# Keys and values of the memory projected in pieces between the steps of two attentions

## The chip, the cores and the metric

The kernel runs on one core of a Trainium2 chip. The metric is the device time of one execution in microseconds (us), as the median of several runs. The program is one launch on that core.

## The reference, cut to what matters

One input x of 256 rows by 1024 passes through two transformer blocks. The part in question is the start of the first block. Everything is float32.

```python
xn = rmsnorm(h, g_mix);  z = xn @ w_in                 # q, k, v: 8 heads of 64; pool input 512; 8 forget logits
fox = forgetting_attention(q, k, v, f_logit)           # causal, with sums of log-sigmoids added to the scores
pool = multiscale_pool(p_in, w_pool, pool_scale)       # trailing means over 2, 4, 8, 16 rows, then a linear map
h = h + concat([fox, pool]) @ w_out

hn = rmsnorm(h, g_mem_q);   mn = rmsnorm(mem, g_mem_kv)
mq  = rmsnorm(heads(hn @ w_mem_q), g_q_mem)            # 4 heads of 128
mkv = mn @ w_mem_kv                                    # first 512 columns: keys, last 512: values
mk  = rmsnorm(heads(mkv[:, :512]), g_k_mem);  mv = heads(mkv[:, 512:])
mo  = softmax(mq @ mk.T / sqrt(128)) @ mv
h = h + mo @ w_mem_out                                 # then the feed-forward layer, and the second block
```

The memory `mem` (256 rows by 1024) is an input of its own: its norm, keys and values depend on nothing that x goes through, and they are first needed by the scores and products of the memory attention.

## The kernel before

Rows stand in two blocks of 128 (`tb` 0 and 1), the 1024 features in eight tiles of 128, or two halves of four. Weights come as slabs of 128 by 2048 floats (1 MB) through a ring of four slots (`NSLOT`): slab n uses slot n modulo 4. SyncE loads it, ScalarE rounds it to a high part (`hi`, L1001), VectorE subtracts to get the low part (`lo`, L1367), and TensorE multiplies. A float32 product is three matmuls on the short type: high by high, high by low, low by high (`mm3`). One slab with both row blocks is 24 matmuls of 512 columns; one projection of 512 columns is two slabs, 48 matmuls. The next load into a slot waits until the old low part is made; the next rounding waits until TensorE has used the old slab. Activations are split in the same way into `x_hi` and `x_lo`.

A norm is: squares on ScalarE (`norm_squares`), mean on VectorE (`x_variance`), the power -1/2 on GpSimd (L407), scaling on VectorE (`x_scale`), transposes on TensorE (`x_transposes`, L416), gain on VectorE (`x_full`), then high part on ScalarE (`x_hi`) and low part on VectorE (`x_low`). `normed_chunk` puts the transposes of the second row block between the first matmuls. `head_norm` does the same per head, with the sum of squares reduced on VectorE.

Nothing is scheduled by a program: each engine has its list of instructions, written out by hand, and takes them in this order. An instruction waits for semaphores, and all that stands behind it on its engine waits too. The order on TensorE before is: memory's norm and its four slabs (keys, then values) with the transposes of the keys; x's norm and the eight slabs of `w_in`, with the forget gates behind the first two; head transposes; pooling (averages, projection); scores of the forgetting attention, first for row block 1, then 0 (`fox_scored`); transposes of the weights, products with the values (`fox_mixed`); the four slabs of `w_out`; the memory query's norm, two slabs, head transposes, scores, transposes, value products (`mem_mixed`); two slabs of `w_mem_out`; and the feed-forward layer. VectorE and ScalarE go along, and split slabs ahead between the steps. `memory attention` means the part from the query's norm to `mem_mixed`, `seam` a place where TensorE has finished a residual's product and waits for the norm of the sum.

Every name `mem_...`, `fox_...` or `x_...` in quotes is a semaphore; some share one counter, in the order of the table `IN_ORDER`.

## Time and profile before

| | us |
|---|---|
| median of 3 runs | 1440.93 |
| lowest and highest | 1439.89, 1443.88 |
| the profiled execution | 1439.54 |
| its span | 1438.2 |
| TensorE matmul busy | 1374.4 (96%) |
| VectorE busy | 966.8 (67%) |
| ScalarE busy | 624.1 (43%) |

The first product starts 15.50 us into the span, and the first product with `w_mem_out` at 207.02. In the timeline a row has its start, its duration, the engine, the line, the operation, what it writes and reads, its shape and how many instructions were merged in it; in brackets stand the time for which the engine was idle before and what ended it. Durations of matmuls overlap, so the distance from one start to the next is what a matmul costs. A float32 matmul that isn't split shows as two rows. In a row of a table by stretches each engine has busy time and count; the granted clock of TensorE is the first number behind POOL's, as a share of 2.4 GHz.

### The profile page before, as it was taken

Reading aid. Unit: us, or ns where it says so; the run is one execution under the profiler, and the core shown is the slowest. Engines: PE = TensorE matmul, PEld = TensorE weight load, DVE = VectorE, ACT = ScalarE, POOL = GpSimd, SP = SyncE. Lnnn points to the kernel's source line nnn. Section 1 sums busy time; section 2 is a strip of 40 time slices with the busy share of each in tenths; the row PEclk is TensorE's granted clock in tenths of the full one; section 3 lists DMA queues with packets and bytes.
Section 4 is the critical chain, followed back from the end, with each engine's and each line's share of the span. In section 5 each row is a group of like instructions: output and inputs, shape, how many; then the busy total and the mean of one; then the engine's idle time right before and its main releaser. Section 6 shows DMA issues by size and latency. Waiting matters only on the chain.

```text
span 1438.2 us, 19599 instructions
## 1 busy us (share of the span) xinstructions
PE 1374.4 (96%) x8222; PEld 1224.7 (85%) x8222; DVE 966.8 (67%) x1543; ACT 624.1 (43%) x535; POOL 35.1 (2%) x31
## 2 busy tenths in 40 slices
PE   6897868999999999899999999999999999999998
PEld 5786657888888888699999999999998888888886
DVE  6434645888846585758887869999546666666664
ACT  5344334434323855344444444444444444444441
POOL 0010010000002000000000000000000000000000
PEclk9899979999988998999999999999999999999999
DMA  7440226899724221355666748888898777777760
GB/s 309 156 170 1 117 85 245 325 375 377 288 96 190 88 89 59 149 191 202 224 234 220 244 169 255 250 253 257 261 319 316 267 294 302 279 290 296 291 263 30
DMA packets 83239, 317.39 MB, mean 221 GB/s; under 512 B 6096, under 2 KB 40144, under 8 KB 53200
## 3 DMA queue, kind: packets, MB, share of 16 engines
q1 hardware_dynamic: 83152, 316.14, 60.9%
q8 instruction: 65, 1.06, 0.3%
q14 instruction: 22, 0.18, 0.0%
HBM read 281.51 MB, written 34.60 MB: 220 GB/s over the span
## 4 chain that ended last, share of the span: by engine, by line
PE 93%; DVE 3%; ACT 3%; issue 0%; DMA 0%; POOL 0%; DVEq 0%; ACTq 0%; POOLq 0%
PE psum L413 91%; PE psum L416 2%; DVE arena L1406 1%; DVE slab_lo L1367 0%; ACT arena L1092 0%; ACT x_hi L1015 0%; DMA arena<-in_mem 0%; POOL statistics L407 0%; ACT slab_hi L1001 0%; DVE residual L1435 0%; ACT arena L1004 0%; DVE arena L1402 0%; DVE arena L1422 0%; DVE statistics L1419 0%; DVE statistics L1511 0%
## 5 line engine op out<-in xcount | busy, mean ns | idle before, releaser
L1367 DVE TENSOR_TENSOR slab_lo<-slab_raw,slab_hi 128x2048 fp32r<-128x2048 f32 x207 | 471.7, 2288 | 250.5 <-ACT slab_hi L1001 240.9
L1001 ACT ACTIVATE slab_hi<-slab_raw 128x2048 fp32r<-128x2048 f32 x207 | 394.1, 1911 | 350.7 <-PE psum L413 350.7
L413 PE MATMUL psum<-x_hi,slab_hi 128*128 128x256 f32 x1184 | 338.3, 286 | 0.9 <-ACT arena L1187 0.9
L413 PE MATMUL psum<-slab_hi,x_hi 128*128 128x512 f32 x784 | 316.3, 403 | 22.5 <-ACT x_hi L1015 13.1
L413 PE MATMUL psum<-x_hi,slab_lo 128*128 128x256 f32 x1184 | 335.2, 283 | 0.0
L413 PE MATMUL psum<-x_lo,slab_hi 128*128 128x256 f32 x1184 | 335.2, 283 | 0.0
L413 PE MATMUL psum<-slab_lo,x_hi 128*128 128x512 f32 x784 | 311.8, 398 | 0.0
L413 PE MATMUL psum<-slab_hi,x_lo 128*128 128x512 f32 x784 | 311.6, 397 | 0.0
L413 PEld LDWEIGHTS psum<-x_hi,slab_hi 128*128 128x128 f32 x1184 | 227.3, 192 | 1.7 <-ACT arena L1187 1.2
L413 PEld LDWEIGHTS psum<-x_lo,slab_hi 128*128 128x128 f32 x1184 | 227.3, 192 | 0.0
L413 PEld LDWEIGHTS psum<-x_hi,slab_lo 128*128 128x128 f32 x1184 | 227.2, 192 | 0.0
L413 PEld LDWEIGHTS psum<-slab_hi,x_hi 128*128 128x128 f32 x784 | 151.6, 193 | 57.5 <-ACT x_hi L1015 14.7
L413 PEld LDWEIGHTS psum<-slab_hi,x_lo 128*128 128x128 f32 x784 | 151.0, 193 | 32.5
L413 PEld LDWEIGHTS psum<-slab_lo,x_hi 128*128 128x128 f32 x784 | 151.5, 193 | 30.9 <-issue 0.2
L413 PE MATMUL psum<-slab_hi,weighted_hi 128*128 128x512 f32 x280 | 109.9, 393 | 1.4 <-DVE weighted_lo L1582 1.4
L413 PE MATMUL psum<-slab_hi,weighted_lo 128*128 128x512 f32 x280 | 109.1, 390 | 0.0
L413 PE MATMUL psum<-slab_lo,weighted_hi 128*128 128x512 f32 x280 | 109.0, 389 | 0.0
L1332 ACT ACTIVATE arena<-psum 128x1024 f32<-128x1024 f32 x32 | 32.8, 1025 | 127.7 <-PE psum L413 127.7
L1923 DVE TENSOR_SCALAR arena<-iota,selected_first_keys,selected_gates 128x128 f32<-128x128 f32 x256 | 86.9, 339 | 0.0
L413 PEld LDWEIGHTS psum<-slab_hi,weighted_hi 128*128 128x128 f32 x280 | 52.6, 188 | 12.2 <-DVE weighted_lo L1582 1.6
L413 PEld LDWEIGHTS psum<-slab_hi,weighted_lo 128*128 128x128 f32 x280 | 52.6, 188 | 11.0
L413 PEld LDWEIGHTS psum<-slab_lo,weighted_hi 128*128 128x128 f32 x280 | 52.6, 188 | 10.5
(233 smaller groups left out, 1188.8 us busy)
## 6 DMA issues: line engine op xcount, KB each, us to landing
slab_raw<-in_ex_u SPq DMA_DIRECT2D x64, 1024.0 KB, 6.1
slab_raw<-in_ex_v SPq DMA_DIRECT2D x64, 1024.0 KB, 4.8
arena<-in_w_ada SPq DMA_DIRECT2D x24, 1024.0 KB, 6.4
slab_raw<-in_w_in SPq DMA_DIRECT2D x22, 1024.0 KB, 5.6
slab_raw<-in_w_gu SPq DMA_DIRECT2D x22, 1024.0 KB, 7.1
hidden_store<-arena SPq DMA_DIRECT2D x32, 512.0 KB, 7.3
gates_store<-arena SPq DMA_DIRECT2D x8, 2048.0 KB, 9.6
arena<-hidden_store SPq DMA_DIRECT2D x32, 512.0 KB, 5.7
```

The lines of the kernel that those rows point to most:

```text
L413: return PE.matmul(out, lhsT, rhs, start=start, stop=stop)
L416: return PE.transpose(out, in_, ident[0:in_.shape[0], 0:in_.shape[0]])
L1001: ACTE.activation(slab_hi[:, slot, :], raw[:, slot, :], ACT.Copy).then_inc(hi_made[slot], 1)
L1332: ACTE.activation(hidden_out[c % 2], banks(2 * (c % 2), 2).rearrange("p (a t) -> p a t", a=EX_A), ACT.Gelu).then_inc(sem("hidden_made"), 1)
L1367: DVE.tensor_tensor(slab_lo[:, slot, :], raw[:, slot, :], slab_hi[:, slot, :].bitcast(f32), ALU.subtract).then_inc(lo_made[slot], 1)
L1406: ins = DVE.tensor_scalar(full[:, k], src[:, k], gain[:, kk:kk + 1], shift[:, kk:kk + 1], ALU.mult, ALU.add)
L1923: ins = DVE.tensor_scalar(gated[n][:, j, :], iota[:], sel_a[:, t], sel_g[:, t], ALU.is_equal, ALU.mult)
```

## The change

The weight slabs come in another order: `w_in` first, then the two slabs of memory's keys (now 8 and 9), `w_out`, `w_mem_q`, the two slabs of memory's values (16 and 17) and `w_mem_out`. The program begins with x. Memory is loaded after the third slab, in one transfer; its norm stands beside the forget gates and in the third slab of `w_in`. The first four of memory's feature tiles are kept in `weighted_hi` and `weighted_lo`; the last four are split twice, for the keys into the first half of `x_hi` and `x_lo`, for the values into the second. The 96 matmuls with memory come in eight pieces of 12 (one slab, one row block): one before and one after the pool's projection, two behind the scores of the forgetting attention, two behind the memory query's projection, one before and one after the memory scores. The keys are copied out of PSUM, normed in place and transposed between the second and third slab of `w_out`. The scores of row block 0 lie closer together in PSUM, so that banks 6 and 7 are free for the pieces. The arena is laid out anew, and the counters are renumbered.

```diff
 def slab_order():
-    order = [("w_mem_kv", j) for j in range(4)] + [("w_in", j) for j in range(8)]
+    order = [("w_in", j) for j in range(8)] + [("w_mem_kv", j) for j in range(2)]
     order += [("w_out", 2 * c + half) for half, c in OUT_ORDER]
-    order += [("w_mem_q", j) for j in range(2)] + [("w_mem_out", j) for j in range(2)]
...
+S_IN, S_MK, S_OUT, S_MQ, S_MV, S_MO, S_FF, S_IN2, S_OUT2, S_PQ, S_EU, S_EV, S_END = (
+    0, 8, 10, 14, 16, 18, 20, 53, 67, 71, 79, 143, 207)
...
-                SP.dma_start(gm[:, tb], a["mem"][:, tb]).then_inc(sem(f"mem_loaded{tb}"), 16)
+                SP.dma_start(h[:, tb], a["x"][:, tb]).then_inc(sem(f"x_loaded{tb}"), 16)
             SP.dma_start(cols[:, 0:192], a["cols"]).then_inc(sem("columns_loaded"), 16)
             SP.dma_start(ident[:], a["ident"]).then_inc(sem("columns_loaded"), 16)
             SP.dma_start(ones[:], a["ones"]).then_inc(sem("columns_loaded"), 16)
             SP.dma_start(iota[:], a["iota"]).then_inc(sem("columns_loaded"), 16)
-            for n in range(4):
+            for n in range(3):
                 load(n)
-            SP.dma_start(h[:], a["x"]).then_inc(sem("x_loaded"), 16)
-            for n in range(4, 8):
-                load(n)
-            SP.wait_ge(*after("x_scaled", 2))
             SP.dma_start(wsm, a["w_f"]).then_inc(sem("forget_weight_loaded"), 16)
             SP.dma_start(fox_mask, a["fox_mask"]).then_inc(sem("block1_constants_loaded"), 16)
             SP.dma_start(upto, a["upto"]).then_inc(sem("block1_constants_loaded"), 16)
             SP.dma_start(bfor, a["b_forget"]).then_inc(sem("block1_constants_loaded"), 16)
-            load(8)
-            load(9)
+            SP.dma_start(gm, a["mem"]).then_inc(sem("mem_loaded"), 16)
+            for n in range(3, 6):
+                load(n)
             SP.wait_ge(*after("x_transposed", 4 * MIX + 4))
             SP.dma_start(bandsT, a["bands"]).then_inc(sem("pool_tables_loaded"), 16)
             SP.dma_start(zs[:, 0:512], a["w_pool"]).then_inc(sem("pool_tables_loaded"), 16)
-            for n in range(10, S_FF + 2):
+            for n in range(6, S_FF + 2):
...
-            normed_chunk(4, S_KV, MEM, 0)
-            gemm_chunk(6, S_KV + 2)
-            PE.wait_ge(*after("mem_k_normed", 1))
-            head_transposes("mem_k_transposed", lambda hh, tb: mkn[:, tb * MEM_H + hh, :], MEM_H, 0, P)
-
-
-            PE.wait_ge(*after("mem_kT_made", 2))
-            PE.wait_ge(*after("mem_v_copied", 1))
             normed_chunk(0, S_IN, MIX, 4)
             PE.wait_ge(*after("forget_weight_lo", 1))
             small_products().then_inc(sem("forget_products_made"), 1)
+            x_transposes(MEM, 4, 0)
             PE.wait_ge(*after("forget_logs_made", 1))
             PE.wait_ge(*after("block1_constants_loaded", 48))
             mm(ps[:, 7, 16:24], upto, fl[:, 0, :])
             mm(ps[:, 7, 24:32], ones[:], fl[:, 0, :], True, False)
             mm(ps[:, 7, 24:32], upto, fl[:, 1, :], False, True).then_inc(sem("forget_sums_made"), 1)
-            gemm_chunk(2, S_IN + 2)
+            for half in range(2):
+                take(S_IN + 2 + half)
+                for tb in range(TB):
+                    half_products(2, S_IN + 2 + half, half, tb)
+                if half == 0:
+                    PE.wait_ge(*after("x_full", 4 * MEM + 2))
+                    x_transposes(MEM, 2, 1)
+            PE.wait_ge(*after("x_full", 4 * MEM + 4))
             gemm_chunk(4, S_IN + 4)
             PE.wait_ge(*after("forget_sums_copied", 1))
             gemm_chunk(6, S_IN + 6)
 
+
+            def memory_products(n, half, tb):
+
+                if half == 0:
+                    ah, al = wh, wl
+                elif n < S_MV:
+                    ah, al = xh[:, 0:4], xl[:, 0:4]
+                else:
+                    ah, al = xh[:, 4:8], xl[:, 4:8]
+                if tb == 0:
+                    take(n)
+                bh, bl = parts(n % NSLOT, 4, 512)
+                for k in range(4):
+                    ins = mm3(ps[:, 6 + tb, :], ah[:, k, tb * P:tb * P + P], al[:, k, tb * P:tb * P + P], bh[:, k], bl[:, k],
+                              half == 0 and k == 0, half == 1 and k == 3)
+                if tb == TB - 1:
+                    used(ins, n)
...
+            PE.wait_ge(*after("fox_kT_made", 4))
+            PE.wait_ge(*after("mem_early_lo", 1))
+            memory_products(S_MK, 0, 0)
             PE.wait_ge(*after("pool_average_copied", 1))
             for g in range(4):
                 ins = mm(ps[:, 2 + g // 2, (g % 2) * S:(g % 2) * S + S], zs[:, g * P:g * P + P], mixT[:, g, :])
             ins.then_inc(sem("pool_projected"), 1)
+            memory_products(S_MK, 0, 1)
...
+            PE.wait_ge(*after("mem_late_lo_for_k", 1))
+            for tb in range(TB):
+                memory_products(S_MK + 1, 1, tb)
...
+            PE.wait_ge(*after("mem_k_normed", 1))
+            head_transposes("mem_k_transposed", lambda hh, tb: mkn[:, tb * MEM_H + hh, :], MEM_H, 4, P)
...
             normed_chunk(0, S_MQ, MEMQ, 4)
+            for tb in range(TB):
+                memory_products(S_MV, 0, tb)
             PE.wait_ge(*after("mem_q_normed", 1))
             head_transposes("mem_q_transposed", lambda hh, tb: mqn[:, tb * MEM_H + hh, :], MEM_H, 2, P)
+            PE.wait_ge(*after("mem_late_lo_for_v", 1))
+            memory_products(S_MV + 1, 1, 0)
             PE.wait_ge(*after("mem_qT_made", 2))
+            PE.wait_ge(*after("mem_kT_made", 2))
...
+            memory_products(S_MV + 1, 1, 1)
             for tb in range(TB):
                 PE.wait_ge(*after("mem_weights_made", tb + 1))
                 for mb in range(TB):
+                    if mb == 1:
+                        PE.wait_ge(*after("mem_exp_made", 2 * MEM_H))
...
-            x_hi(MEM, 0)
+                ACTE.wait_ge(*after(f"x_loaded{tb}", 16))
+                norm_squares(MIX, 0, tb)
+            x_hi(MIX, 0)
             hi(0, 1)
-            x_hi(MEM, 1)
-            hi(2, 3)
-            ACTE.wait_ge(*after("x_loaded", 16))
-            for tb in range(TB):
-                norm_squares(MIX, 2, tb)
-            hi(4, 5)
-            slab_done(ACTE, S_KV + 1)
-            ACTE.wait_ge(*after("x_lo_made", 4 * MEM + 4))
-            ACTE.activation(mksq, banks(4, 2).rearrange("p (h d) -> p h d", d=MEM_D), ACT.Square).then_inc(
-                sem("mem_k_squared"), 1)
-            slab_done(ACTE, S_KV + 3)
-            ACTE.activation(mv, ps[:, 6:8, :], ACT.Copy).then_inc(sem("mem_v_copied"), 1)
-            ACTE.wait_ge(*after("columns_loaded", 64))
-            heads_out("mem_k_transposed", mkT, MEM_H, 0, P, cols[:, C_MEMK:C_MEMK + 1], "mem_kT_made")
-
-
-            for tb in range(TB):
-                x_hi(MIX, tb)
+            x_hi(MIX, 1)
             ACTE.wait_ge(*after("forget_weight_loaded", 16))
             ACTE.activation(wsm_h[:], wsm, ACT.Copy).then_inc(sem("forget_weight_hi"), 1)
-            hi(6, 7)
+            hi(2)
+            for tb in range(TB):
+                ACTE.wait_ge(*after("mem_loaded", 16))
+                norm_squares(MEM, 2, tb)
+            hi(3, 4, 5)
+            slab_done(ACTE, S_IN + 1)
+            ACTE.wait_ge(*after("x_lo_made", x_part(MIX, 1, 1)))
+            ACTE.activation(qsq, banks(0, 2).rearrange("p (h d) -> p h d", d=FOX_D), ACT.Square).then_inc(
+                sem("fox_q_squared"), 1)
             ACTE.wait_ge(*after("forget_added", 1))
             log_sigmoid_rest(fl, fe).then_inc(sem("forget_rest_made"), 1)
-            hi(8, 9)
-            slab_done(ACTE, S_IN + 1)
-            ACTE.wait_ge(*after("x_lo_made", 4 * MIX + 4))
-            ACTE.activation(qsq, banks(0, 2).rearrange("p (h d) -> p h d", d=FOX_D), ACT.Square).then_inc(
-                sem("fox_q_squared"), 1)
-            hi(10, 11)
+            hi(6)
+            ACTE.wait_ge(*after("x_full", 4 * MEM + 3))
+            ACTE.activation(wh[:], mem_early, ACT.Copy).then_inc(sem("mem_early_hi"), 1)
...
+            ACTE.wait_ge(*after("x_full", 4 * MEM + 4))
+            ACTE.activation(xh[:, 0:4], mem_late, ACT.Copy).then_inc(sem("mem_late_hi_for_k"), 1)
...
+            slab_done(ACTE, S_MK + 1)
+            ACTE.activation(mkn.rearrange("p (b h) d -> p b (h d)", b=TB), ps[:, 6:8, :], ACT.Copy).then_inc(
+                sem("mem_k_copied"), 1)
...
-            hi(14, 15, 16, 17)
+            ACTE.wait_ge(*after("mem_k_copied", 1))
+            ACTE.activation(mksq, mkn, ACT.Square).then_inc(sem("mem_k_squared"), 1)
+            hi(12, 13)
+            ACTE.wait_ge(*after("columns_loaded", 64))
+            heads_out("mem_k_transposed", mkT, MEM_H, 4, P, cols[:, C_MEMK:C_MEMK + 1], "mem_kT_made")
+            hi(14, 15)
...
+            ACTE.activation(xh[:, 4:8], mem_late, ACT.Copy).then_inc(sem("mem_late_hi_for_v"), 1)
+            hi(18)
...
+            slab_done(ACTE, S_MV + 1)
+            ACTE.activation(mv, ps[:, 6:8, :], ACT.Copy).then_inc(sem("mem_v_copied"), 1)
...
-            hi(20, 21)
+            hi(19, 20, 21)
...
+            def memory_low(name, dst, hi_, full):
+                DVE.wait_ge(*after(name.replace("_lo", "_hi"), 1))
+                DVE.tensor_tensor(dst, full, hi_.bitcast(f32), ALU.subtract).then_inc(sem(name), 1)
...
+            lo(2)
+            k = [x_variance(MEM, 2, tb) for tb in range(TB)]
+            for tb in range(TB):
+                x_scale(MEM, 2, tb, k[tb])
...
+            for half in range(2):
+                x_full(MEM, 4, 0, half, cols[:, CKV:CKV + 8], None)
...
-            lo(14, 15, 16, 17)
+            lo(12)
+            head_norm("mem_k", mkn, mkn, 8, MEM_D, 40, mksq, (13,))
+            lo(14, 15)
...
+            lo(16, 17)
+            head_norm("mem_q", banks(0, 2).rearrange("p (h d) -> p h d", d=MEM_D), mqn, 8, MEM_D, 8, mqsq,
+                      (lambda: memory_low("mem_late_lo_for_v", xl[:, 4:8], xh[:, 4:8], mem_late),))
+            lo(18)
...
-            lo(20, 21)
+            lo(19, 20, 21)
```

TensorE, from the head transposes of the forgetting attention to its first scores. `arena` holds the activations, `hidden` here the pool's weights, `weighted_hi` and `weighted_lo` in the changed kernel the early half of memory. Before:

```order
L416 MATMUL psum<-ident,arena 66x128 x32
L413 MATMUL psum<-arena 128x256 x8
L413 MATMUL psum<-arena,hidden 128x256 x4
L413 MATMUL psum<-arena 128x256
L413 MATMUL psum<-arena,ident 128x128
```

Changed, the same place:

```order
L421 MATMUL psum<-ident,arena 66x128 x32
L418 MATMUL psum<-arena 128x256 x8
L418 MATMUL psum<-slab_hi,weighted_hi 128x512
L418 MATMUL psum<-slab_lo,weighted_hi 128x512
L418 MATMUL psum<-slab_hi,weighted_lo 128x512
...
L418 MATMUL psum<-arena,hidden 128x256 x4
L418 MATMUL psum<-slab_hi,weighted_hi 128x512
L418 MATMUL psum<-slab_lo,weighted_hi 128x512
L418 MATMUL psum<-slab_hi,weighted_lo 128x512
...
L418 MATMUL psum<-arena 128x256
L418 MATMUL psum<-arena,ident 128x128
```

A piece of 12 matmuls (the three shown, four times) now stands on either side of the pool's projection.

VectorE, from the copy of the forgetting attention's transposed weights to the first sum of the residual. The reductions and `statistics` belong to the norm of the keys. Before:

```order
L1522 COPY arena<-psum 128x1024
L1525 COPY arena<-psum 128x1024
L1527 TENSOR_TENSOR x_lo<-arena,x_hi 128x1024
L1367 TENSOR_TENSOR slab_lo<-slab_raw,slab_hi 128x2048 x4
L1435 TENSOR_TENSOR residual<-residual,psum 128x1024
```

Changed, the same place:

```order
L1580 COPY arena<-psum 128x1024
L1583 COPY arena<-psum 128x1024
L1585 TENSOR_TENSOR x_lo<-arena,x_hi 128x1024
L1415 TENSOR_TENSOR slab_lo<-slab_raw,slab_hi 128x2048
L1471 TENSOR_REDUCE statistics<-arena 128x8
L1421 TENSOR_SCALAR statistics<-statistics 128x8
L1415 TENSOR_TENSOR slab_lo<-slab_raw,slab_hi 128x2048
L1474 TENSOR_TENSOR arena<-arena,statistics 128x1024
L1415 TENSOR_TENSOR slab_lo<-slab_raw,slab_hi 128x2048 x2
L1487 TENSOR_TENSOR residual<-residual,psum 128x1024
```

The norm of the keys stands between the splits of slabs 12 to 15, of which four were in a row before.

## Rows read from the trace of the kernel before

**Rows 1.** The page, chain of work that ended last: shares by engine

```profile
PE 93%; DVE 3%; ACT 3%; issue 0%; DMA 0%; POOL 0%; DVEq 0%; ACTq 0%; POOLq 0%
```

**Rows 2.** Timeline of TensorE, 15 to 207.5 us: its first product, then waits

```profile
15.50 0.76 PE L413 MATMUL psum<-slab_hi,x_hi 128*128 128x512 f32 x1 [5.66 <-DVE slab_lo L1367]
...
42.99 1.09 PE L416 MATMUL psum<-ident,arena 128*128 128x128 f32 x8 [1.29 <-ACT arena L1021]
...
45.87 0.47 PE L413 MATMUL psum<-slab_hi,x_hi 128*128 128x512 f32 x1 [1.78 <-ACT x_hi L1015]
...
65.85 0.60 PE L413 MATMUL psum<-arena 128*128 128x8 f32 x2 [1.22 <-DVE arena L1481]
...
110.45 1.99 PE L413 MATMUL psum<-arena,hidden 128*128 128x256 f32 x8 [1.11 <-ACT arena L1083]
...
113.76 0.48 PE L413 MATMUL psum<-arena 66*128 66x256 f32 x1 [1.31 <-DVE arena L1502]
...
128.32 5.11 PE L416 MATMUL psum<-ident,arena 128*128 128x128 f32 x24 [5.47 <-ACT arena L1092]
...
134.64 2.84 PE L413 MATMUL psum<-arena 128*64 128x256 f32 x32 [1.21 <-ACT arena L1097]
...
163.40 0.47 PE L413 MATMUL psum<-slab_hi,x_hi 128*128 128x512 f32 x1 [3.05 <-ACT x_hi L1015]
...
182.60 1.97 PE L416 MATMUL psum<-ident,arena 128*128 128x128 f32 x8 [5.55 <-DVE arena L1422]
...
185.34 6.54 PE L413 MATMUL psum<-arena 128*128 128x256 f32 x16 [0.78 <-ACT arena L1021]
...
194.54 3.78 PE L416 MATMUL psum<-ident,arena 128*128 128x128 f32 x16 [2.66 <-DVE arena L1546]
...
199.64 3.72 PE L413 MATMUL psum<-arena 128*128 128x256 f32 x16 [1.32 <-DVE arena L1549]
...
207.02 0.50 PE L413 MATMUL psum<-slab_hi,x_hi 128*128 128x512 f32 x1 [3.66 <-DVE x_lo L1554]
```

**Rows 3.** Timeline of TensorE: groups and single matmuls that give prices

```profile
57.72 0.17 PE L413 MATMUL psum<-small_weight_hi,x_hi 128*128 128x8 f32 x1
...
69.00 0.63 PE L413 MATMUL psum<-slab_lo,x_hi 128*128 128x512 f32 x1
...
69.43 0.63 PE L413 MATMUL psum<-slab_hi,x_lo 128*128 128x512 f32 x1
...
101.99 3.65 PE L416 MATMUL psum<-ident,arena 128*66 128x128 f32 x32
...
105.64 3.69 PE L413 MATMUL psum<-arena 128*128 128x256 f32 x16
...
139.36 0.39 PE L413 MATMUL psum<-slab_hi,x_lo 128*128 128x512 f32 x1
...
139.59 0.39 PE L413 MATMUL psum<-slab_hi,x_hi 128*128 128x512 f32 x1
```

**Rows 4.** Stretches: busy time of each engine, granted clock, DMA

```profile
61.30:65.00 3.70, 3.33 (x17) 3.24 (x16) 0.17 (x1) 0.12 (x1) 0.00 (x0) 0.51 0.28 115
102.00:109.30 7.30, 7.30 (x49) 6.34 (x47) 0.00 (x0) 5.61 (x9) 0.00 (x0) 1.00 0.18 73
128.30:130.00 1.70, 1.68 (x8) 1.70 (x9) 1.34 (x2) 0.00 (x0) 0.00 (x0) 0.50 0.00 0
```

**Rows 5.** Timelines of VectorE and ScalarE, 137 to 183 us

```profile
137.53 1.22 DVE L1525 COPY arena<-psum 128x1024 f32<-128x1024 f32 x1 [6.00 <-PE psum L413]
...
141.68 2.29 DVE L1367 TENSOR_TENSOR slab_lo<-slab_raw,slab_hi 128x2048 fp32r<-128x2048 f32 x1 [0.58 <-ACT slab_hi L1001]
...
178.14 1.22 DVE L1419 TENSOR_REDUCE statistics<-arena 128x8 f32<-128x1024 f32 x1 [1.40 <-ACT arena L1110]
...
181.32 1.22 DVE L1422 TENSOR_TENSOR arena<-psum,statistics 128x1024 f32<-128x1024 f32 x1 [1.76 <-POOL statistics L407]
...
139.75 3.71 ACT L1001 ACTIVATE slab_hi<-slab_raw 128x2048 fp32r<-128x2048 f32 x2
```

More of the change, by code:

```diff
@@ L73, in slab_order @@
 def slab_order():
-    order = [("w_mem_kv", j) for j in range(4)] + [("w_in", j) for j in range(8)]
+    order = [("w_in", j) for j in range(8)] + [("w_mem_kv", j) for j in range(2)]
     order += [("w_out", 2 * c + half) for half, c in OUT_ORDER]
-    order += [("w_mem_q", j) for j in range(2)] + [("w_mem_out", j) for j in range(2)]
+    order += [("w_mem_q", j) for j in range(2)] + [("w_mem_kv", j) for j in range(2, 4)]
+    order += [("w_mem_out", j) for j in range(2)]
     order += [("w_gu", 0), ("w_gu", 1)]
@@ L344, in sync_program @@
             n0 = S_FF + 2 + 3 * (FF_N - 1)
-            SP.wait_ge(*after("x_lo_made", 4 * FFN + 4))
+            SP.wait_ge(*after("x_lo_made", x_part(FFN, 1, 1)))
             for name in c2:
@@ L351, in sync_program @@
                 if n == S_IN2 + 6:
-                    SP.wait_ge(*after("x_lo_made", 4 * MIX2 + 4))
+                    SP.wait_ge(*after("x_lo_made", x_part(MIX2, 1, 1)))
                     SP.dma_start(zs[:], a["g_out"]).then_inc(sem("output_gains_loaded"), 16)
@@ L432, in x_ready @@
             def x_ready(norm, tb, half):
-                PE.wait_ge(*after("x_hi_made", 4 * norm + 2 * tb + half + 1))
-                PE.wait_ge(*after("x_lo_made", 4 * norm + 2 * tb + half + 1))
+                PE.wait_ge(*after("x_hi_made", x_part(norm, tb, half)))
+                PE.wait_ge(*after("x_lo_made", x_part(norm, tb, half)))
             def x_transposes(norm, bank, tb):
@@ L571, in tensor_program @@
             PE.wait_ge(*after("fox_weightsT_copied", 4))
+            PE.wait_ge(*after("mem_k_copied", 1))
             for hh in range(FOX_H):
@@ L600, in tensor_program @@
             PE.wait_ge(*after("mem_pT_copied", 2))
+            PE.wait_ge(*after("mem_v_copied", 1))
             for hh in range(MEM_H):
@@ L1374, in rstd @@
                                   ALU.add).then_inc(sem("variance_made"), 1)
-                lo(*between)
+                for part in between:
+                    if callable(part):
+                        part()
+                    else:
+                        lo(part)
                 DVE.wait_ge(*after("rstd_made", k))
@@ L1389, in x_low @@
             def x_low(norm, tb, half):
-                DVE.wait_ge(*after("x_hi_made", 4 * norm + 2 * tb + half + 1))
+                DVE.wait_ge(*after("x_hi_made", x_part(norm, tb, half)))
                 four, rows = slice(4 * half, 4 * half + 4), slice(tb * P, tb * P + P)
@@ L1468, in vector_program @@
             ins.then_inc(sem("query_gains_scaled"), 1)
-            for tb in range(TB):
-                x_split(MIX, 4, tb, cols[:, CM:CM + 8])
-            DVE.wait_ge(*after("forget_weight_hi", 1))
-            DVE.tensor_tensor(wsm_l[:], wsm, wsm_h[:].bitcast(f32), ALU.subtract).then_inc(sem("forget_weight_lo"), 1)
-            lo(6, 7)
+            lo(3, 4)
             DVE.wait_ge(*after("forget_products_made", 1))
@@ L1484, in vector_program @@
                 sem("forget_sums_copied"), 1)
-            lo(8, 9)
+            lo(5)
+            for half in range(2):
+                x_full(MEM, 2, 1, half, cols[:, CKV:CKV + 8], None)
+            memory_low("mem_early_lo", wl[:], wh[:], mem_early)
+            lo(6)
             qa_v = qa.rearrange("p b h d -> p (b h) d")
```

93 lines of the change are left out of this document (48 added, 45 removed).

## The prediction

> **What bounds the kernel now.** I read the page first. TensorE holds 93% of the chain that ended last [rows 1], so only two things can shorten this program: TensorE waiting less, or TensorE running at its full clock more. The diff neither removes nor adds a product; it moves them. The DMA section is not needed for the bound, as no wait of TensorE between its first product and 207 us ends at a transfer. Next I read TensorE's timeline up to the output projection of the memory attention, whose first matmul starts at 207.02. Behind that point the two programs have the same order, except for one slab split. Thirteen waits stand there [rows 2], together 30.4 us: 1.29+1.78 around the seam between memory and x, 1.22 for the forget logs, 1.11+1.31 around the pooling, 5.47 for the softmax, 1.21, 3.05, 5.55 for the query norm, 0.78, 2.66, 1.32, 3.66. Then I read the granted clock. After the wait of 5.47 us it stands at 0.50 [rows 4], the lower of its two levels (1.2 of 2.4 GHz), and after the wait of 5.55 us 8 transposes take 1.97 us [rows 2], as they would there. A 512-column matmul starts every 0.227 us at the upper level and every 0.427 at the lower one [rows 3]. So a long wait is paid twice.
>
> **Prices at full clock** [rows 3]: 12 slab matmuls 2.7 us, 24 5.45, 48 10.9. 32 transposes take 3.65, so 24 cost 2.75, 16 1.8 and 8 0.9 to 1.0; 16 rows of 256 columns 3.7. At the lower clock the same 24 transposes took 5.11, 16 took 3.78, 8 took 1.97 and the 16 rows of the memory scores 6.54 [rows 2]: 2.4, 2.0, 1.0 and 2.8 us too much, 8.2 in all.
>
> **The sum, as a walk along TensorE after the change.** The head is alike: x comes in the two half transfers in which memory came, so I keep 15.50 as the first matmul's start [rows 2].
> - x's first chunk: 12 matmuls at the lower clock 5.1, transposes 0.8, 36 matmuls 8.2: ends 29.6.
> - Forget products: 57.72 to 65.85 is 8.13 with its 1.22 wait [rows 2, 3], so 6.8 of work: 36.4. Here the clock has fallen, as it had at the end of these products before (0.51, [rows 4]), so memory's 8 transposes take about 1.8. VectorE puts two multiplications of 0.68 behind them and ahead of the forget logs, so the sums start at 39.3. That is a wait of about 1.0, where it was 1.22: the transposes cover nothing, because what they feed stands ahead of the logs on VectorE.
> - Sums and 144 matmuls: 101.99 less 65.85 is 36.1, plus 8 transposes 0.8: 76.3. The splits keep ahead; the tightest, slab 7, is split near 63 and wanted at 71.
> - Head transposes and pool averages: 3.65 and 3.69 [rows 3], 7.3: 83.6. Piece of 12, projection (8 rows, 1.9), piece of 12: 90.9. ScalarE's copy and VectorE's scaling (1.0 and 1.2 us) lie under the pieces: both pooling waits go.
> - Scores 9.0, to 99.9. From the first score to the first transpose was 128.32 less 113.76, 14.56 [rows 2]: allowed at 105.5. Two pieces (5.45) fill that to 105.35. Wait 0.1 instead of 5.47, and the clock has no cause to fall.
> - 24 transposes at full clock 2.75. ScalarE's four copies start only when the last third is written and after memory's keys are copied (1.0): a wait of 1.6 to 1.7. Value products 2.8: end 112.7. 48 matmuls: 123.6.
> - **New wait.** VectorE copies the fox result (1.2), ScalarE rounds it (1.1), squares the keys (about 1.0, like its other passes over 1024 columns), rounds slab 12 (1.9); VectorE splits slab 12 (2.2), reduces (1.2), splits slab 13 (2.2), multiplies (1.2) [rows 5]. From 112.7 this ends at 125.1: TensorE waits 1.5. Bounds: 0 if the square starts early, 3.5 if each handover costs 0.2 us more; I take 1.5. Behind it stand 8 transposes (1.0) and the last 48 output products: 137.0. Behind VectorE's work stand slabs 14 and 15, split until 133.4; the first rows' residual is ready at 131.7. Its sum is 1.5 late, and TensorE pays 0.1 to 0.2 of that at the seam.
> - Seam to the memory query: 3.05 of wait and 1.0 of transposes, now 4.2: 141.2. Query chunk as before, 182.60 less 5.55 less 163.40, 13.6: 154.8 (its own first matmuls stay slow).
> - Query norm: two pieces' worth, 24 matmuls, 5.45 under a chain of 5.55: wait 0.1, then 8 transposes at full clock: 161.4. Piece 2.7, scores 3.7, piece 2.7: 170.5. VectorE's maximum and ScalarE's four exponentials (1.2+1.9) and normalisation (1.4) run under the last piece up to 170.8.
> - Two groups of transposes with waits of 0.3 and 1.0 (the second block's weights): 173.6. Copies 1.35, products 3.7, and the wait for the output's halves 3.7: 182.3.
> - Slab 19 is now split behind that point. Its low part is ready 2.9 us after the start, and TensorE first has 12 slow matmuls of slab 18, over 4 us. Three splits instead of two end some 2.2 us later; before, VectorE then stood idle, and what is late is a first-rows sum with 0.7 us of slack. Cost 0, at most 1.
>
> 207.0 less 182.3 is 24.7. The cross-check: waits fall from 30.4 to about 13.7 (16.7), clock gives 8.2 less 0.9 for memory's transposes (7.3), and the removed stops also save their restart, some 0.1 to 0.2 us each.
>
> The profiled execution took 1439.54, span 1438.2, and 1439.54 less 24.7 is 1414.8. The median shown is 1.4 above that execution, so I say 1415.5.
>
> **A rule that speaks against it.** The trace: 32 transposes in 3.6 us were granted 1.00 throughout, and so were the pool averages after them [rows 3, 4]; but the 48 forget products of 8 columns ended at the lower clock [rows 4]. The Trainium skill, "TensorE: Matmul & The Clock Gate", part 4 (PE-mode transpose), says that transposes do not count as TensorE being busy, as matmuls do. By that the two places where transposes stand between waits (105.5 to 112.7 and 170.8 to 175.0) would lose the clock. No row of before shows such a place reached at full clock: the stretch from 128.32 to 137.42 was entered at 0.50 and left at full clock, although a third of it was transposes and waits. That makes the rule's result a rival and not the forecast.
>
> **The rivals.**
> 1. The clock falls in one or both thin places. The price is about 8.5 slab matmuls at 0.427 instead of 0.227, 1.7 us, behind the first. Behind the second it is up to 3.7, if the 16 rows run slow as the memory scores did. Time 1417.5 to 1421. For: the waits of 1.6, 1.0 and 1.35 stand among transposes. Against: waits of 1.29, 1.78, 1.11 and 1.31 did not bring the clock down [rows 2].
> 2. The pieces cover less than planned, because ScalarE and VectorE are in order and got more between the attention's steps (copies of keys and values, two more roundings and subtractions of 1.0 to 1.2, slabs 11, 12, 13 and 18). If each of the six steps named above slips by one such operation (1.1), 6.6 comes back; with one wait long enough for the clock also its 1.7 to 2.8. Time 1421 to 1428. For: the new wait above, and 0.1 us of margin at both large waits. Against: both engines are half idle there.
> 3. **Slower.** Pieces cut small between attention steps never bring the clock back: from the first piece at 83.6 on, the 240 slab matmuls up to 182 start every 0.427, 0.2 us more each, 48 us. That gives 1463 in full, and it decides from the point where more than half of them (24.7 of 48) run slow. Against: behind the transposes and waits from 128.32 on, the slab matmuls were fast at 139.4 [rows 3]. It would have to be a behaviour that no row shows.
> 4. Better: the keys' norm is not waited for and memory's transposes run fast: 2.4 less, 1412.5.
>
> **Chances.** Forecast (1412.5 to 1417.5) 0.64, rival 1 0.21, rival 2 0.09, better 0.04, rival 3 and anything at or above no change 0.02. The range 1412 to 1420.5 leaves out the tail of rival 1 and rivals 2 and 3, about 0.15. A difference under 0.3% (4.3 us) cannot be told from none here; only something between rivals 2 and 3 falls there. Faster 0.97, same 0.02, slower 0.01.
>
> **What would show it.** In the profile after: the first output product of the memory attention starts near 182.3; no TensorE wait over 2 us from 84 to 137; a granted clock of 1.00 from 42 to 137, and from 148 until the copies near 175; a new wait of about 1.5 in front of four rows of head transposes near 124, released by VectorE's multiplication into the arena; the query seam still near 3 us and slow behind it. I am wrong if a 5 us wait is still there, if the span behind the memory attention changes length, or if the first x chunk starts later than 15.5.

## The result, and the profile after

| | before | after |
|---|---|---|
| median, us | 1440.41 (4 runs) | 1419.39 (4 runs, 1417.75 to 1419.48) |
| span of the profiled execution | 1438.2 | 1418.0 |
| first product with `w_mem_out` starts at | 207.02 | 186.78 |

The changed kernel takes 0.9843 of the time before (95% interval 0.9829 to 0.9856), 21.0 us less. Forecast were 1415.5 us, 25.4 less than the median then known; the range, 1412.0 to 1420.5, holds the time. The narrower band of the likeliest case, 1412.5 to 1417.5, does not: 1419.39 lies in the band of rival 1. One run of the kernel before, 3498.31 us, in the session of experiments 1 to 4, is left out of the ratios given there. The profiled spans differ by 20.2 us, and TensorE's first product with `w_mem_out` comes 20.24 earlier: the gain lies where it was looked for.

The page of the changed kernel: the shares by engine of the chain that ended last, to be read beside [rows 1].

```profile
PE 93%; DVE 4%; ACT 2%; POOL 1%; issue 0%; DMA 0%; ACTq 0%; DVEq 0%; POOLq 0%
```

TensorE still holds it. Here is TensorE's timeline of the changed kernel, as in [rows 2]: start, duration, what, and in brackets the wait and who ended it.

```profile
15.22 0.76 PE L418 MATMUL psum<-slab_hi,x_hi 128*128 128x512 f32 x1 [5.66 <-DVE slab_lo L1415]
...
38.32 0.60 PE L418 MATMUL psum<-arena 128*128 128x8 f32 x2 [0.86 <-DVE arena L1533]
...
104.54 2.81 PE L421 MATMUL psum<-ident,arena 128*128 128x128 f32 x24
...
108.89 2.84 PE L418 MATMUL psum<-arena 128*64 128x256 f32 x32 [1.55 <-issue]
...
125.51 1.09 PE L421 MATMUL psum<-ident,arena 128*128 128x128 f32 x8 [2.67 <-DVE arena L1474]
...
143.03 0.47 PE L418 MATMUL psum<-slab_hi,x_hi 128*128 128x512 f32 x1 [3.05 <-ACT x_hi L1058]
...
163.15 1.09 PE L421 MATMUL psum<-ident,arena 128*128 128x128 f32 x8 [1.03 <-DVE arena L1474]
...
166.84 3.61 PE L418 MATMUL psum<-arena 128*128 128x256 f32 x16
...
173.48 1.09 PE L421 MATMUL psum<-ident,arena 128*128 128x128 f32 x8 [0.29 <-DVE arena L1608]
...
175.31 1.09 PE L421 MATMUL psum<-ident,arena 128*128 128x128 f32 x8 [0.73 <-DVE arena L1608]
...
177.71 5.41 PE L418 MATMUL psum<-arena 128*128 128x256 f32 x16 [1.32 <-DVE arena L1611]
...
186.78 0.50 PE L418 MATMUL psum<-slab_hi,x_hi 128*128 128x512 f32 x1 [3.66 <-DVE x_lo L1616]
```

The two waits around the seam between memory and x and the two around the pooling are gone. The wait of 5.47 ahead of the 24 transposes has no bracket left, and they take 2.81 instead of 5.11; the wait of 5.55 for the query's norm is 1.03. Together the nine waits shown behind the first product are 15.2 us, where thirteen were 30.4. The other 5.0 of the 20.2 us are mostly clock: 2.3 at these 24 transposes and 2.9 at the memory scores (166.84, 3.61 for 6.54) are the largest gains, with losses against them at the keys and the value products.

Three rows are worse than the forecast. The keys' transposes at 125.51 wait 2.67 us (forecast 1.5), the query's head transposes at 163.15 wait 1.03 (forecast 0.1), and the value products at 177.71 take 5.41 where 3.72 stood in [rows 2].

The granted clock in four stretches of the changed kernel (busy time by engine, then the clock behind POOL's): the transposes of the weights with the products behind them, the output products behind the keys' transposes, the value products of the memory attention, and the first matmuls of the feed-forward layer.

```profile
104.50:112.00 7.50, 5.95 (x58) 5.32 (x58) 2.71 (x4) 3.10 (x5) 0.00 (x0) 1.00 0.01 2
127.00:129.00 2.00, 2.00 (x6) 1.52 (x6) 0.00 (x0) 2.00 (x2) 0.00 (x0) 0.50 0.00 0
177.80:181.00 3.20, 3.20 (x8) 2.55 (x9) 0.00 (x0) 0.00 (x0) 0.00 (x0) 0.50 0.00 0
203.50:205.00 1.50, 1.47 (x7) 1.24 (x8) 1.19 (x2) 0.00 (x0) 0.00 (x0) 1.00 1.00 421
```

From 104.5 to 112 the clock is 1.00, though transposes, a wait of 1.55 and narrow products stand there. It is 0.50 behind the new wait and in the value products. At 203.5, behind the same wait of 3.05 us as before the change, it is 1.00, where it fell to the lower level before; that gave 1.6 us, and the same amount was lost again between 392 and 404 us, in instructions that the change does not touch.

### The profile page after: what moved, and what is told of

It reads as the page before. It is cut to its first block, busy times and chain, and to the rows that moved or that the text cites. A ratio compares the mean times of both kernels' runs of the same rounds, so it can differ in the third digit from the quotient of the medians.

```text
span 1418.0 us, 19593 instructions
## 1 busy us (share of the span) xinstructions
PE 1369.8 (97%) x8222; PEld 1220.4 (86%) x8222; DVE 967.4 (68%) x1542; ACT 625.5 (44%) x535; POOL 37.9 (3%) x31
## 4 chain that ended last, share of the span: by engine, by line
PE 93%; DVE 4%; ACT 2%; POOL 1%; issue 0%; DMA 0%; ACTq 0%; DVEq 0%; POOLq 0%
PE psum L418 91%; PE psum L421 2%; DVE slab_lo L1415 1%; POOL statistics L412 1%; DVE arena L1458 1%; ACT slab_hi L1044 0%; DMA residual<-in_x 0%; ACT x_hi L1058 0%; ACT arena L1164 0%; DVE arena L1474 0%; DVE residual L1487 0%; DVE statistics L1471 0%; ACT arena L1047 0%; DVE arena L1454 0%; DVE arena L1985 0%
## 5 line engine op out<-in xcount | busy, mean ns | idle before, releaser
L418 PE MATMUL psum<-slab_hi,x_hi 128*128 128x512 f32 x768 | 311.1, 405 | 20.7 <-ACT x_hi L1058 11.3
L418 PE MATMUL psum<-slab_hi,x_lo 128*128 128x512 f32 x768 | 305.8, 398 | 0.0
L418 PE MATMUL psum<-slab_lo,x_hi 128*128 128x512 f32 x768 | 305.6, 398 | 0.0
L418 PE MATMUL psum<-slab_hi,weighted_hi 128*128 128x512 f32 x296 | 116.9, 395 | 1.4 <-DVE weighted_lo L1644 1.4
L418 PE MATMUL psum<-slab_lo,weighted_hi 128*128 128x512 f32 x296 | 115.9, 392 | 0.0
L418 PE MATMUL psum<-slab_hi,weighted_lo 128*128 128x512 f32 x296 | 115.9, 392 | 0.0
L418 PEld LDWEIGHTS psum<-slab_hi,weighted_hi 128*128 128x128 f32 x296 | 56.0, 189 | 12.9 <-DVE weighted_lo L1644 1.6
L418 PEld LDWEIGHTS psum<-slab_hi,weighted_lo 128*128 128x128 f32 x296 | 56.0, 189 | 11.7
L418 PEld LDWEIGHTS psum<-slab_lo,weighted_hi 128*128 128x128 f32 x296 | 55.9, 189 | 11.3
```

The source lines that it names most:

```text
L418: return PE.matmul(out, lhsT, rhs, start=start, stop=stop)
```

## The experiments

Each time below is a median. Experiments 1 to 4 are compared with the first measurement of the changed kernel, 1419.39, which was not repeated beside them; experiments 5 to 7 with its repetition beside them, 1419.11 (experiment 8). Starts of single instructions are those of one profiled execution each. These already differ by up to 0.5 us where the programs are still the same, so for experiments 1, 2, 4, 5 and 6 the text says how much of a shift stood ahead of the edit.

**1. Slab 13 split behind the keys' norm.**

```diff
-            head_norm("mem_k", mkn, mkn, 8, MEM_D, 40, mksq, (13,))
-            lo(14, 15)
+            head_norm("mem_k", mkn, mkn, 8, MEM_D, 40, mksq)
+            lo(13, 14, 15)
```

> Slab 13's split moves from inside the keys' norm (between VectorE's variance and its multiplication) to behind it. Theory A: GpSimd's power on 8 numbers took 3.61 us because a 2.28 us VectorE pass over SBUF runs at the same time; alone it takes about 1.65, as in the kernel before. Then TensorE's wait ahead of the keys' transposes falls from 2.67 to about 0.7 us, the clock stays up behind it (48 matmuls in 10.9 instead of 12.7), of this 0.5 comes back at the seam: about 3.3 us faster than the changed kernel, 1416. Theory B: the power is slow there for another reason: wait still 2.2 to 2.7, no gain (and slab 13 comes later). Theory C: only the clock is independent of the wait: 1.6 to 2 us faster, with slow matmuls still behind the transposes.

Measured: 1416.45 us (1413.86 to 1417.15), ratio to before 0.9823 (0.9807 to 0.984), 2.9 less than the changed kernel, whose fastest run was 1417.75. VectorE and GpSimd of the changed kernel around this norm:

```profile
120.33 0.17 DVE L1421 TENSOR_SCALAR statistics<-statistics 128x8 f32<-128x8 f32 x1
...
120.41 2.28 DVE L1415 TENSOR_TENSOR slab_lo<-slab_raw,slab_hi 128x2048 fp32r<-128x2048 f32 x1
...
124.22 1.23 DVE L1474 TENSOR_TENSOR arena<-arena,statistics 128x1024 f32<-128x1024 f32 x1 [1.53 <-POOL statistics L412]
...
120.58 3.61 POOL L412 TENSOR_TENSOR statistics<-statistics,minus_half 128x8 f32<-128x8 f32 x1 [54.18 <-DVE statistics L1421]
```

And with slab 13 behind it:

```profile
120.61 0.17 DVE L1421 TENSOR_SCALAR statistics<-statistics 128x8 f32<-128x8 f32 x1
...
122.53 1.23 DVE L1474 TENSOR_TENSOR arena<-arena,statistics 128x1024 f32<-128x1024 f32 x1 [1.75 <-POOL statistics L412]
...
123.67 2.29 DVE L1415 TENSOR_TENSOR slab_lo<-slab_raw,slab_hi 128x2048 fp32r<-128x2048 f32 x1
...
120.86 1.64 POOL L412 TENSOR_TENSOR statistics<-statistics,minus_half 128x8 f32<-128x8 f32 x1 [54.14 <-DVE statistics L1421]
...
123.81 1.09 PE L421 MATMUL psum<-ident,arena 128*128 128x128 f32 x8 [0.69 <-DVE arena L1474]
```

The same power on 8 numbers takes 3.61 us beside VectorE's pass over two SBUF operands and 1.64 without it. The pass had begun first (120.41); it ends at 122.69, and the power ends 1.5 us later, as if it had started only then. TensorE's wait falls to 0.69 and the 48 matmuls behind it from 12.74 to 11.15. Theory A holds, B falls: the wait goes, and `w_mem_out` starts 3.15 us earlier (183.63 for 186.78), although this execution was 0.3 later ahead of the edit.

The kernel before already had such a place, on 16 numbers, which the prediction does not use. Here are GpSimd and VectorE of the kernel before:

```profile
446.51 4.88 POOL L407 TENSOR_TENSOR statistics<-statistics,minus_half 128x16 f32<-128x16 f32 x1 [21.27 <-DVE statistics L1373]
...
456.98 2.90 POOL L407 TENSOR_TENSOR statistics<-statistics,minus_half 128x16 f32<-128x16 f32 x1 [5.58 <-DVE statistics L1373]
...
446.34 2.29 DVE L1367 TENSOR_TENSOR slab_lo<-slab_raw,slab_hi 128x2048 fp32r<-128x2048 f32 x1
...
457.27 2.29 DVE L1367 TENSOR_TENSOR slab_lo<-slab_raw,slab_hi 128x2048 fp32r<-128x2048 f32 x1 [0.37 <-ACT slab_hi L1001]
```

Where the pass began first, the power took 4.88. Where the power began first, it took 2.90, the same as alone (2.90 at 73.33), and the pass took its usual 2.29. Nor does every pass of VectorE hold the power up. In the changed kernel a power on one number at 141.81 took 0.56, as alone, beside a pass with one of its operands in PSUM that had begun at 141.65. The Trainium skill, "SBUF — State Buffer", section "SBUF: two separate sides", states this: VectorE and GpSimd share a pair of SBUF ports as an exclusive lock, which a VectorE operation with two SBUF inputs, if it starts first, takes for its whole length against a GpSimd operation that reads SBUF. The trace agrees: 3.61 against 1.64. In the same section the Trainium skill says that the lock works the other way too, when GpSimd starts first; the row at 457.27 does not show that.

**2. The values' low part behind the query's norm.**

```diff
-            head_norm("mem_q", banks(0, 2).rearrange("p (h d) -> p h d", d=MEM_D), mqn, 8, MEM_D, 8, mqsq,
-                      (lambda: memory_low("mem_late_lo_for_v", xl[:, 4:8], xh[:, 4:8], mem_late),))
+            head_norm("mem_q", banks(0, 2).rearrange("p (h d) -> p h d", d=MEM_D), mqn, 8, MEM_D, 8, mqsq)
+            memory_low("mem_late_lo_for_v", xl[:, 4:8], xh[:, 4:8], mem_late)
```

> The subtraction for the values' late half moves from inside the query's norm to behind it. Theory A (GpSimd is held up by VectorE's pass): the power takes 1.65 instead of 2.55, TensorE's wait of 1.03 ahead of the query's head transposes falls to about 0.1; 0.7 to 0.9 us faster. Theory B (not held up): the power stays at 2.5, no change or up to 0.5 slower.

Measured: 1419.51 us (1418.34 to 1419.86). In the changed kernel GpSimd's power began 0.17 us after the start of VectorE's pass of 1.22 us (159.11):

```profile
159.28 2.55 POOL L412 TENSOR_TENSOR statistics<-statistics,minus_half 128x8 f32<-128x8 f32 x1 [16.91 <-DVE statistics L1421]
```

TensorE and GpSimd of this experiment's kernel:

```profile
161.87 1.09 PE L421 MATMUL psum<-ident,arena 128*128 128x128 f32 x8
...
158.91 1.65 POOL L412 TENSOR_TENSOR statistics<-statistics,minus_half 128x8 f32<-128x8 f32 x1 [16.88 <-DVE statistics L1421]
...
185.81 0.50 PE L418 MATMUL psum<-slab_hi,x_hi 128*128 128x512 f32 x1 [3.66 <-DVE x_lo L1616]
```

The power takes 1.65, and the wait has no bracket left: the mechanism of theory A, now at a second place. `w_mem_out` starts 0.97 earlier than in the changed kernel, but 0.34 of that stood already at the seam to the query (142.69 for 143.03), ahead of the edit. The edit's part is 0.6, as the pieces behind the transposes now wait some 0.3 for the values' low part. The profiled execution, the fastest of the five, ended 1.0 ahead of the changed kernel's; the medians show no gain. A gain of 0.6 cannot be told in them: the runs of either kernel differ by more.

**3. The keys' norm ahead of the fox result.**

```diff
-            ACTE.wait_ge(*after("foxT_copied", 1))
-            ACTE.activation(xh[:, 0:4], foxT, ACT.Copy).then_inc(sem("fox_x_hi"), 1)
             ACTE.wait_ge(*after("mem_k_copied", 1))
             ACTE.activation(mksq, mkn, ACT.Square).then_inc(sem("mem_k_squared"), 1)
-            hi(12, 13)
+            hi(12)
+            ACTE.wait_ge(*after("foxT_copied", 1))
+            ACTE.activation(xh[:, 0:4], foxT, ACT.Copy).then_inc(sem("fox_x_hi"), 1)
+            hi(13)
...
+            head_norm("mem_k", mkn, mkn, 8, MEM_D, 40, mksq)
             DVE.wait_ge(*after("fox_mixed", 1))
...
-            lo(12)
-            head_norm("mem_k", mkn, mkn, 8, MEM_D, 40, mksq, (13,))
-            lo(14, 15)
+            lo(12, 13, 14, 15)
```

> ScalarE squares the keys and rounds slab 12 ahead of its wait for the fox result, VectorE norms the keys ahead of that wait. Theory A: the wait of 2.67 us is the chain of in-order work behind the fox result; it goes to 0, the clock stays up, 0.6 comes back at the seam: 3.9 us faster than the changed kernel, about 1415.5. Theory B (VectorE is the bound there, the work is only moved): the wait for the fox result's low half takes its place, under 1.5 us gained.

Measured: 1413.08 us (1412.81 to 1414.65), ratio to before 0.9809 (0.9793 to 0.9825), 6.3 less than the changed kernel, more than theory A gave. VectorE and TensorE of this kernel:

```profile
109.84 1.22 DVE L1472 TENSOR_REDUCE statistics<-arena 128x8 f32<-128x1024 f32 x1 [2.74 <-ACT arena L1139]
...
113.01 1.23 DVE L1475 TENSOR_TENSOR arena<-arena,statistics 128x1024 f32<-128x1024 f32 x1 [1.75 <-POOL statistics L412]
...
114.15 1.22 DVE L1585 COPY arena<-psum 128x1024 f32<-128x1024 f32 x1
...
122.79 1.03 PE L421 MATMUL psum<-ident,arena 128*128 128x128 f32 x8
...
135.07 1.09 PE L421 MATMUL psum<-ident,arena 128*128 128x128 f32 x8 [0.35 <-DVE arena L1439]
...
138.81 0.47 PE L418 MATMUL psum<-slab_hi,x_hi 128*128 128x512 f32 x1 [2.64 <-ACT x_hi L1058]
...
171.87 3.72 PE L418 MATMUL psum<-arena 128*128 128x256 f32 x16 [1.32 <-DVE arena L1611]
...
179.26 0.80 PE L418 MATMUL psum<-slab_hi,x_hi 128*128 128x512 f32 x1 [3.67 <-DVE x_lo L1616]
```

VectorE norms the keys in time in which it stood idle before; the fox result is copied 2.4 us later (114.15 for 111.77), and nobody waits for that. The keys' transposes start without a wait. Up to 179.26 the gain is 7.5: the wait 2.7, 1.6 for 48 matmuls at full clock, 1.6 for the query's first 12, 1.7 for value products that took 3.72. The last two are clock that the expectation had not counted, and nothing here ties them to the edit; 1.0 is lost again in the 48 matmuls with `w_mem_out` (13.66 us for 12.67 to the transposes behind them). So theory A has the wait and the clock behind it right, and the rest of the gain is clock that neither theory had foreseen.

**4. Filler in the wait ahead of the value products.** Six matmuls more, whose result is not used.

```diff
-            PE.wait_ge(*after("mem_pT_copied", 2))
             PE.wait_ge(*after("mem_v_copied", 1))
+            take(S_MO)
+            fh, _ = parts(S_MO % NSLOT, 4, 512)
+            for i in range(6):
+                mm(ps[:, 6 + i % 2, :], xh[:, 4, 0:P], fh[:, i % 4])
+            PE.wait_ge(*after("mem_pT_copied", 2))
```

> Six extra matmuls of 512 columns into a free bank stand in the 1.32 us wait ahead of memory's value products (extra work, its result is not used). Theory A: those products ran at the lower clock (5.41 us for 16 rows, 3.72 before) because TensorE had little work in the 4 us ahead of them; with the filler they take 3.7: 1.5 us faster. Theory B: the clock's fall is decided earlier, or by the transposes: products still 5.4, 0 to 0.2 slower.

Measured: 1418.13 us (1417.24 to 1420.49), 1.3 less by median, with ranges that overlap. Its profiled execution was the slowest of the five; it was 1.4 us ahead of the changed kernel's at `w_mem_out` (185.39) and 1.2 behind at the end. Two rows of TensorE, and the clock behind them:

```profile
126.03 1.09 PE L421 MATMUL psum<-ident,arena 128*128 128x128 f32 x8 [2.63 <-DVE arena L1478]
...
178.01 3.72 PE L418 MATMUL psum<-arena 128*128 128x256 f32 x16
```

```profile
127.50:129.50 2.00, 2.00 (x11) 1.63 (x10) 0.00 (x0) 2.00 (x2) 0.00 (x0) 1.00 0.00 0
178.10:181.70 3.60, 3.60 (x16) 2.87 (x16) 0.00 (x0) 0.00 (x0) 0.00 (x0) 1.00 0.00 0
```

The value products take 3.72 at full clock, as theory A says. But they also did in experiment 3, without any filler, so this run does not prove the filler's part. And at 127.5 the clock is 1.00 behind a wait of 2.63, where it was 0.50 in the changed kernel behind 2.67, with the same instructions on all engines up to there; this execution ran 0.5 us later by then (the weights' transposes began at 105.05 for 104.54).

**5. The key pieces behind the transposes instead of behind the scores.**

```diff
-            PE.wait_ge(*after("mem_late_lo_for_k", 1))
-            for tb in range(TB):
-                memory_products(S_MK + 1, 1, tb)
             PE.wait_ge(*after("fox_weights_made", 1))
...
+            PE.wait_ge(*after("mem_late_lo_for_k", 1))
+            for tb in range(TB):
+                memory_products(S_MK + 1, 1, tb)
             PE.wait_ge(*after("fox_late_weightsT_copied", 1))
```

ScalarE's copy of the keys moves behind its four copies of the weights.

> The two key pieces (24 matmuls) that stand behind the scores of the forgetting attention move behind the transposes of its weights, ScalarE's copy of the keys behind its copies of those weights. Theory A (the pieces' gain is the softmax wait that they cover plus the clock that they keep): the wait of 5.5 us is back ahead of the 24 transposes, these take 5.1 instead of 2.8, the pieces now cover the 1.55 us wait for the copies: 6 to 7 us slower than the changed kernel, 1425 to 1426.5. Theory B (only the wait counts, the clock is noise): 3.9 slower, 1423.3. Theory C (the chain through ScalarE and VectorE sets the time there, the pieces cover nothing on the path): under 1 us.

Measured: 1425.98 us (1423.98 to 1427.15), 6.9 more than the changed kernel beside it. TensorE of this kernel:

```profile
104.99 5.35 PE L421 MATMUL psum<-ident,arena 128*128 128x128 f32 x24 [5.49 <-ACT arena L1128]
...
117.17 2.84 PE L418 MATMUL psum<-arena 128*64 128x256 f32 x32 [1.21 <-ACT arena L1136]
...
109.10 2.07 ACT L1133 ACTIVATE arena<-psum 128x512 f32<-128x512 f32 x4 [4.25 <-PE psum L421]
...
116.00 1.02 ACT L1136 ACTIVATE arena<-psum 128x1024 f32<-128x1024 f32 x1 [4.84 <-PE psum L418]
```

The wait of 5.49 is back and the transposes take 5.35; the products with the values start at 117.17, 8.3 later than in the changed kernel (108.89), of which 0.4 stood ahead of the edit (VectorE's reduction behind the scores began at 99.54 for 99.10). The rest, 7.8, is more than expected for two reasons. The pieces began at the lower clock (5.98 from the first start to the last end, for 5.72 in the changed kernel). And, the larger part, the move made a wait of its own. The four copies of the weights end at 111.17, under the pieces, so their wait of 1.55 is covered; the 1.21 is for ScalarE's copy of the keys (L1136 in this kernel), out of the banks that the products write next. Behind that, memory's value products take 3.72 instead of 5.41, which gives 1.7 back, and the 48 matmuls with `w_mem_out` take 1.1 more. Theory A holds; B's 1423.3 lies below all six runs.

**6. The first value pieces behind the query's head transposes.**

```diff
-            for tb in range(TB):
-                memory_products(S_MV, 0, tb)
             PE.wait_ge(*after("mem_q_normed", 1))
...
+            for tb in range(TB):
+                memory_products(S_MV, 0, tb)
             PE.wait_ge(*after("mem_late_lo_for_v", 1))
```

> The two value pieces (24 matmuls) behind the memory query's projection move behind the query's head transposes. Theory A: a wait of 6.6 us stands ahead of these transposes (5.55 before the change, 1.1 more since GpSimd's power is held up), they take 2.0 instead of 1.1, and the first 8 or so matmuls behind them run at the lower clock, 1.7 more: 8 to 8.5 us slower than the changed kernel, 1427.5. Theory B (clock not affected): 5.6 slower, 1425. Theory C (as for the keys, nothing covered): under 1 us.

Measured: 1425.68 us (1424.88 to 1427.01), 6.6 more.

```profile
163.69 1.97 PE L421 MATMUL psum<-ident,arena 128*128 128x128 f32 x8 [6.47 <-DVE arena L1474]
...
185.89 3.72 PE L418 MATMUL psum<-arena 128*128 128x256 f32 x16 [1.32 <-DVE arena L1611]
```

The wait is 6.47 and the transposes take 1.97; the value products start 8.2 later than in the changed kernel, but take 3.72 for 5.41. At the seam to the query, ahead of the edit, this execution was already 0.5 later (143.55 for 143.03), so the move itself cost 7.7 up to there: theory A's path (8 to 8.5), slightly less, and not B's 5.6. Of it 1.7 is given back by the clock at the value products. The expected total was too high by 1.8.

**7. Experiments 2 and 3 together.** The edits are those shown.

> The early keys' norm (1413.1 alone) together with the values' subtraction behind the query's norm. If the second edit is worth its wait of 1.03 less 0.05 for the new one, 0.9 us on the path: 1412.2. If its gain is lost in the clock's play (the edit alone measured 1419.5, no gain): 1413.

Measured: 1412.89 us (1410.72 to 1414.96), ratio to before 0.9797 (0.9775 to 0.9819). That cannot be told from experiment 3 alone. It is the fastest version by median, 6.2 us below the changed kernel beside it. TensorE of this kernel:

```profile
138.67 0.47 PE L418 MATMUL psum<-slab_hi,x_hi 128*128 128x512 f32 x1 [2.65 <-ACT x_hi L1058]
...
157.88 1.09 PE L421 MATMUL psum<-ident,arena 128*128 128x128 f32 x8
```

The query's wait of 1.03 is gone here too (157.88). But from the seam to the matmul behind the query's second transposes TensorE took 1.6 us longer than in experiment 3 (138.67 to 143.90, for 138.81 to 142.43), because part of that ran at the lower clock here and none of it there. Up to there that hides the gain, as the second expectation had it.

**8. The changed kernel again.**

> The changed kernel itself, for a time on the same chip and a second profile. Theory A: the clock behind short waits (2.67 ahead of the keys' transposes, 1.32 ahead of the value products) differs from one execution to the next: 1417.5 to 1419.5, and in this profile one of the places (48 matmuls behind the keys' transposes, value products, first matmuls of the FFN) has the other level. Theory B: it is set by the program: the same levels at all of them.

Measured: 1419.11 us (1418.43 to 1419.79). TensorE of this execution:

```profile
125.68 1.09 PE L421 MATMUL psum<-ident,arena 128*128 128x128 f32 x8 [2.67 <-DVE arena L1474]
...
177.91 5.41 PE L418 MATMUL psum<-arena 128*128 128x256 f32 x16 [1.32 <-DVE arena L1611]
...
186.98 0.49 PE L418 MATMUL psum<-slab_hi,x_hi 128*128 128x512 f32 x1 [3.66 <-DVE x_lo L1616]
```

Waits and durations are those of the first profile at all places looked at. That favours theory B, but it is two executions only, and all nine runs of the changed kernel have the same mean granted clock, 0.979. The kernel before behaves otherwise: over its eleven runs beside this one the mean granted clock goes from 0.975 to 0.968 and the time from 1438.53 to 1447.62 us, by and large the longer the lower the clock. So levels need not repeat for one program. What the runs do show is that the wait alone does not fix the level behind it: waits of 1.32, of 2.64 to 2.65 and of 3.05 us were each followed by both levels, in one program or another, and each such place is worth 1.6 to 1.7 us. What decides it is left open.

## Why the prediction was right, and where it was short

The likeliest case was right in sign, in place and in most of its mechanism. Its sum was 24.7 for the first product with `w_mem_out`, and 20.2 was measured there. The time ended in the band that had been given to rival 1, by a longer wait as well as by the clock.

Of its signs three failed: a TensorE wait over 2 us stands between 84 and 137 (2.67), the clock is not 1.00 throughout there (0.50 at 127), and `w_mem_out` starts at 186.78, not near 182.3. The sign that the span behind the memory attention keeps its length came true (1231.2 us in both), but partly by luck, as 1.6 gained at 203.5 and 1.6 lost near 400 cancel.

- **The head and the x chunk.** As walked: the transposes of memory cover nothing there (wait 0.86 for 1.0), and the head transposes start at 75.65 (forecast 76.3). Up to the end of the fox products TensorE is 1.0 us ahead of the walk, mostly because fewer of the forget products ran at the lower clock (29.70 to 35.49, 5.8 us). The 6.8 allowed for them should have been 6.9 (8.13 less 1.22).
- **Pooling and softmax waits.** Right: neither pooling wait is left, and the pieces end as the last exponential does. Experiment 5 shows both halves of that price, the wait and the clock.
- **The new wait ahead of the keys' transposes.** The wait was forecast, and this is the term that was mis-sized: 1.5 by the sum, 2.67 measured, and 1.7 more as the 48 matmuls behind it took 12.58 from the first start to what follows (126.36 to 138.94), for 10.9. The step that failed is "reduces (1.2), splits slab 13 (2.2), multiplies (1.2)": it took GpSimd's power as hidden under the split, where the power ends only 1.5 us behind the split. Experiment 1 shows it. (The terms of this chain also add up to 12.0, where the walk has 12.4, from 112.7 to 125.1.) Experiment 3 shows that the 0.7 us of wait that experiment 1 leaves come from the chain's place behind the fox result; what it gained beyond that is mostly clock at two later places.
- **The query norm.** The pieces cover it; 1.03 remained for 0.1, from the same cause (2.55 for 1.65, experiment 2).
- **The seam to the query and slab 19.** The seam is 3.05 plus transposes, as forecast. VectorE's first-rows sum behind slab 21 is at 194.54, without delaying TensorE: cost 0.
- **The value products.** 5.41 for 3.7: rival 1 at its second place, at 1.7 us, where up to 3.7 had been allowed. At its first place (105.5 to 112.7) the rival did not come: the clock stayed at 1.00.
- **Rivals 2 and 3.** Every cover but the two named held, and the small pieces ran at full clock.

In sums: 1.2 and 1.7 at the keys, 0.9 at the query's norm, 1.7 at the value products, less the 1.0 ahead, is 4.5, which is what was missing at 186.78. The rule that transposes do not count as work for the clock was given as a rival. The Trainium skill, "TensorE: Matmul & The Clock Gate", part 4, is not borne out at the place where transposes were entered at full clock (104.5 to 112: granted 1.00); behind shorter waits in the memory attention the clock fell in some programs and not in others, which neither supports nor refutes it.

## What to carry to other kernels

Independent products placed in the waits of an attention are worth the wait and, where it was 5 to 6 us long as here, the clock behind it: moving a block of 24 matmuls out of its wait cost 6.6 to 6.9 us. The next thing to look at is the in-order queue of the other engines: work for the independent branch belongs where its engine stands idle ahead of its next wait, not behind it. And a small GpSimd step on the path wants no VectorE pass over two SBUF operands begun just before it. Last, a gain of 1 or 2 us is read from the place of the edit, not from the total, because one place where the clock differs is worth as much.

## What the runs showed of the hardware

- GpSimd's power on 8 numbers took 1.64 to 1.65 us alone, 2.55 beside a VectorE pass of 1.22 and 3.61 beside one of 2.28: each time it ended 1.5 us behind the pass, which had begun first. On 16 numbers it took 4.88 beside a pass that had begun first, and 2.90 where the power began first.
- 24 transposes entered at full clock, a wait of 1.55 and 2.84 us of narrow products left the clock at full.
- Behind equal waits (3.05 us) the next 12 slab matmuls took 4.57 at one place and 3.01 at another in one execution.
- Eleven runs of the kernel before, beside experiments 5 to 8, took 1438.53 to 1447.62 us at mean granted clocks of 0.975 to 0.968.
